# Sliding-window attention in float32: the value product written as three float32r passes over split operands, and a slope pass left out where its operand is zero

## What is computed

```python
def sliding_window_attention(q, k, v, sinks, slopes):
    # blocks of 128 tokens; kk and vv hold the previous block and this one
    logits = jnp.einsum('bnqkgd,bnskd->bnkgqs', qb, kk).astype(jnp.float32) * scale
    logits = logits - sl * dist.astype(jnp.float32)
    logits = jnp.where(valid[None, :, None, None], logits, -jnp.inf)
    p = jax.nn.softmax(jnp.concatenate([logits, sink], axis=-1), axis=-1)[..., :-1]
    out = jnp.einsum('bnkgqs,bnskd->bnqkgd', p.astype(v.dtype), vv)

def odd_layer(h, w_in, b_in, sinks, w_out):
    proj = h @ w_in + b_in
    q, k, v, g = jnp.split(proj, ODD_SPLITS, axis=-1)
    o = sliding_window_attention(q, k, v, sinks, alibi_slopes(SW_HEADS))
    return (o * jax.nn.silu(g)) @ w_out
```

## Time and profile before

| | us |
|---|---|
| median of 3 runs | 1840.45 (1839.17 to 1842.74) |
| the profiled execution, whole | 1845.26 |
| its span, first to last instruction | 1843.5 |
| PE busy | 1673.8 (91% of the span) |
| DVE busy | 1060.7 (58%) |
| ACT busy | 823.3 (45%) |
| the head loop: first scores to last value product | 1647 to 1768 |

### The profile page before, as it was taken

How to read it: one execution, slowest core, us unless ns; L and a number is a source line. 1 busy time by engine, 2 the same in 40 slices (tenths; PEclk the granted TensorE clock), 3 DMA queues, 4 the chain that set the end, 5 groups by cost and what they waited for, 6 DMA issues and landing times.

```text
span 1843.5 us, 24067 instructions
## 1 busy us (share of the span) xinstructions
PE 1673.8 (91%) x8860; PEld 1412.3 (77%) x8860; DVE 1060.7 (58%) x1760; ACT 823.3 (45%) x1544; POOL 93.4 (5%) x112
## 2 busy tenths in 40 slices
PE   7998999998999999989999998889987979979977
PEld 6886787886778888868798896668765758859965
DVE  5557877674545656552254438864465984446654
ACT  5545665663334455541132226652353542235641
POOL 2000400000000000000000001100000100000001
PEclk9998999999999999999999999988997989989988
DMA  6411122113431333322223320111320111320011
GB/s 184 125 50 30 46 63 64 46 52 110 141 120 47 101 104 91 91 92 67 99 74 99 108 81 25 35 46 41 102 84 21 47 46 47 99 69 24 28 42 46
DMA packets 147870, 132.95 MB, mean 72 GB/s; under 512 B 8560, under 2 KB 142448, under 8 KB 147776
## 3 DMA queue, kind: packets, MB, share of 16 engines
q1 hardware_dynamic: 143744, 119.58, 21.3%
q0 software_dynamic: 3136, 10.78, 1.6%
q10 hardware_dynamic: 896, 1.32, 0.3%
HBM read 124.33 MB, written 7.34 MB: 71 GB/s over the span
## 4 chain that ended last, share of the span: by engine, by line
PE 74%; DVE 15%; ACT 5%; issue 5%; DMA 1%; DVEq 0%; ACTq 0%; POOL 0%
PE bank L292 19%; PE bank L293 19%; PE bank L294 19%; DVE wlo L285 2%; PE bank L1206 2%; PE bank L1220 2%; ACT whi L278 1%; PE bank L1189 1%; PE bank L2911 1%; DVE ptl L1374 1%; DVE sz L2700 1%; PE bank L2870 1%; PE bank L1223 1%; PE bank L2278 1%; PE bank L2883 1%
## 5 line engine op out<-in xcount | busy, mean ns | idle before, releaser
L292 PE MATMUL bank<-hh,whi 128*128 128x512 f32 (+3 forms) x1208 | 466.2, 386 | 16.0 <-DVE wlo L285 5.6
L293 PE MATMUL bank<-hl,whi 128*128 128x512 f32 (+3 forms) x1208 | 455.7, 377 | 0.0
L294 PE MATMUL bank<-hh,wlo 128*128 128x512 f32 (+3 forms) x1208 | 455.2, 377 | 0.0
L278 ACT ACTIVATE whi<-wraw 128x2048 fp32r<-128x2048 f32 x111 | 212.1, 1913 | 338.6 <-PE bank L294 338.5
L285 DVE TENSOR_TENSOR wlo<-wraw,whi 128x2048 fp32r<-128x2048 f32 x111 | 254.1, 2289 | 178.7 <-ACT whi L278 177.3
L292 PEld LDWEIGHTS bank<-hh,whi 128*128 128x128 f32 (+2 forms) x1208 | 231.2, 191 | 60.9 <-issue 5.8
L294 PEld LDWEIGHTS bank<-hh,wlo 128*128 128x128 f32 (+2 forms) x1208 | 230.5, 191 | 43.3
L293 PEld LDWEIGHTS bank<-hl,whi 128*128 128x128 f32 (+2 forms) x1208 | 231.2, 191 | 39.1 <-issue 0.7
L1374 DVE TENSOR_TENSOR ptl<-bank,pth 128x128 fp32r<-128x128 f32 (+3 forms) x128 | 56.8, 485 | 64.4 <-ACT pth L1282 63.0
L292 PE MATMUL bank<-ah,whi 128*128 128x512 f32 (+1 forms) x224 | 83.8, 374 | 10.6 <-DVE al L3046 8.3
L292 PE MATMUL bank<-yh,whi 128*128 128x512 f32 (+1 forms) x220 | 79.3, 360 | 6.7 <-DVE yl L1740 6.7
(11 more groups left out here) (393 smaller groups left out, 3212.2 us busy)
## 6 DMA issues: line engine op xcount, KB each, us to landing
wraw<-in_w_in_a_dram SPq DMA_DIRECT2D x52, 512.0 KB, 4.5
wraw<-in_w_up_dram SPq DMA_DIRECT2D x42, 512.0 KB, 4.9
wraw<-in_w_in_dram SPq DMA_DIRECT2D x34, 512.0 KB, 4.8
wraw<-in_w_in_c_dram SPq DMA_DIRECT2D x18, 512.0 KB, 4.7
wraw<-in_w_down_dram SPq DMA_DIRECT2D x16, 512.0 KB, 4.0
wraw<-in_w_out_a_dram SPq DMA_DIRECT2D x16, 512.0 KB, 4.0
aside<-stage POOLq DMA_DIRECT2D x20, 256.0 KB, 2.3
wraw<-in_w_attn_br_dram SPq DMA_DIRECT2D x8, 512.0 KB, 4.0
```

The lines of the kernel that those rows point to most:

```text
L278: act.activation(whi[:, p], wraw[:, p], ACT.Copy).then_inc(w_hi_done, 1)
L292: pe.matmul(out, ws[0], hs[0], start=first, stop=False)
L293: pe.matmul(out, ws[0], hs[1], start=False, stop=False)
L294: return pe.matmul(out, ws[1], hs[0], start=False, stop=last)
```

## The change

Four edits:

1. The value product becomes three float32r passes. The values are written whole into `v3` by one DVE instruction; ACT copies them into `vph3` and DVE subtracts into `vpl3` (two instructions each); POOL zeroes only the columns between. The transposed probabilities are split as they leave PSUM: ACT copies bank 4 and then bank 5 into `pth3`, DVE subtracts each into `ptl3`. `values` waits for both subtractions and issues 12 matmuls in place of four.
2. `queries_low` moves on DVE ahead of the work on the transposed probabilities (`ptl3`), where it stood behind it (`pt3`).
3. The second slope pass and its diagonal are left out for the heads whose slope equals its high part (`exact`): the eight odd ones.
4. Two relays are dropped (`dt_v`, `k3_done`): DVE waited for its own result and then raised a semaphore for another engine, which now waits for the result's own semaphore. PE waits for `v3_pad` and `v3_low` ahead of the head loop, where DVE waited for `v3_pad`.

```diff
-            act.wait_ge(dt_v, 1)
+            act.wait_ge(drained, m0 + 13)
...
-            dve.wait_ge(drained, m0 + 13)
-            dve.sem_inc(dt_v, 1)
...
-            pool.memset(vp3[:, :, :], 0.0).then_inc(v3_pad, 1)
+            pool.wait_ge(drained, m0)
+            for part in (vph3, vpl3):
+                for a in range(0, 5 * HD, 2 * HD):
+                    ins = pool.memset(part[:, :, a:a + HD].bitcast(F32), 0.0)
+            ins.then_inc(v3_pad, 1)
...
-            pe.wait_ge(k3_done, 1)
+            pe.wait_ge(drained, m0 + 1)
...
             act.activation(dist3[:, :], dist3f[:, :], ACT.Copy).then_inc(c4_ready, 1)
+            act.wait_ge(drained, m0 + 2)
+            for g in range(2):
+                act.activation(vph3[:, :, HD + P * g:P + P * g], v3[:, :, HD * g:HD * g + HD], ACT.Copy) \
+                    .then_inc(v3_high, 1)
...
-            dve.wait_ge(drained, m0 + 1)
-            dve.sem_inc(k3_done, 1)
             split_lo(dve, n0 + 2)
             dve.wait_ge(tiles, 2 * n0 + 2)
-            dve.wait_ge(v3_pad, 1)
             dve.wait_ge(got_con, CON4)
-            for tt in range(TT):
-                dst = vp3[:, tt, HD:HD + 256].rearrange("p (g e) -> p g e", g=2)[:, :, 0:HD]
-                ins = dve.tensor_tensor(dst, bank[1][:, P * tt:P * tt + P].rearrange("p (g d) -> p g d", g=2),
-                                        bv3[:, :].rearrange("p (g d) -> p g d", g=2), ALU.add)
-            ins.then_inc(drained, 1)
+            dve.tensor_tensor(v3[:, :, :], bank[1][:, :].rearrange("p (t d) -> p t d", t=TT),
+                              bv3[:, :].unsqueeze(1).to_broadcast([P, TT, P]), ALU.add).then_inc(drained, 1)
+            for g in range(2):
+                cols = slice(HD + P * g, P + P * g)
+                dve.wait_ge(v3_high, g + 1)
+                dve.tensor_tensor(vpl3[:, :, cols], v3[:, :, HD * g:HD * g + HD], vph3[:, :, cols].bitcast(F32),
+                                  ALU.subtract).then_inc(v3_low, 1)
             dve.tensor_scalar(nsink[:, :], pcol("sinks", n=NH), -1.0, None, ALU.mult).then_inc(ns_done, 1)
             for g in range(2):
                 dve.wait_ge(kd3_done, g + 1)
@@ -2844,6 +2853,11 @@
         gated[0] += 1
         QB = NH // 2 + DA_H
...
+        TURNED = ((0, 0, 3 * P), (1, 3 * P, 4 * P))
+
+        def exact(h):
+            return high_part(sl[h]) == sl[h]
...
+            pe.wait_ge(v3_pad, 1)
+            pe.wait_ge(v3_low, 2)
...
-                    pe.matmul(out, dg3[:, h % 2, 0, :], dist3[:, lo:2 * P], start=False, stop=False)
-                    pe.matmul(out, dg3[:, h % 2, 1, :], dist3[:, lo:2 * P], start=False, stop=True).then_inc(s_done, 1)
+                    mm = pe.matmul(out, dg3[:, h % 2, 0, :], dist3[:, lo:2 * P], start=False, stop=exact(h))
+                    if not exact(h):
+                        mm = pe.matmul(out, dg3[:, h % 2, 1, :], dist3[:, lo:2 * P], start=False, stop=True)
+                    mm.then_inc(s_done, 1)
...
                     if i % 2 == 0 and h:
-                        pe.wait_ge(t3_dve if i else t3_act, h)
+                        pe.wait_ge(t3_dve, 2 * h if i else 2 * h - 1)
...
-                pe.wait_ge(t3_act, h + 1)
-                pe.wait_ge(t3_dve, h + 1)
+                pe.wait_ge(t3_dve, 2 * h + 2)
...
-                    mm = pe.matmul(bank[6][:, P * j:P * j + n], vp3[:, j, c0:c0 + P],
-                                   pt3[:, h % 2, 2 * P * j:2 * P * j + n], start=(e == 0 and j == 0),
-                                   stop=(e == 1 and j == TT - 1), skip_group_check=True)
+                    for v, p in ((vph3, pth3), (vpl3, pth3), (vph3, ptl3)):
+                        mm = pe.matmul(bank[6][:, P * j:P * j + n], v[:, j, c0:c0 + P],
+                                       p[:, h % 2, 2 * P * j:2 * P * j + n],
+                                       start=(e == 0 and j == 0 and v is vph3 and p is pth3),
+                                       stop=(e == 1 and j == TT - 1 and p is ptl3), skip_group_check=True)
                 mm.then_inc(pv_done, 1)
...
-                act.activation(dg3[:, h % 2, 0, :], ident[:, :], ACT.Copy, scale=hi_)
-                act.activation(dg3[:, h % 2, 1, :], ident[:, :], ACT.Copy, scale=sl[h] - hi_).then_inc(dg3_done, 1)
+                ins = act.activation(dg3[:, h % 2, 0, :], ident[:, :], ACT.Copy, scale=hi_)
+                if not exact(h):
+                    ins = act.activation(dg3[:, h % 2, 1, :], ident[:, :], ACT.Copy, scale=sl[h] - hi_)
+                ins.then_inc(dg3_done, 1)
...
                 if 1 <= h <= NH:
                     v = h - 1
-                    act.wait_ge(t_done, T3 + 2 * v + 1)
                     if v >= 2:
                         act.wait_ge(pv_done, V3 + v - 1)
-                    act.activation(pt3[:, v % 2, 0:3 * P], bank[4][:, 0:3 * P], ACT.Copy).then_inc(t3_act, 1)
+                    for b, c0, n in TURNED:
+                        act.wait_ge(t_done, T3 + 2 * v + b + 1)
+                        act.activation(pth3[:, v % 2, c0:c0 + n], bank[4 + b][:, 0:n], ACT.Copy).then_inc(t3_act, 1)
                 if h % 2 and h >= 3:
                     out_pair(h // 2 - 1)
                 if h % 2 == 0 and h // 2 + 1 < NH // 2:
@@ -3015,12 +3037,15 @@
                     for i in range(TT):
                         part = pr3[:, v % 2, i, (P if i == 0 else 0):2 * P]
                         dve.tensor_scalar(part, part, rs3[:, v % 2, i:i + 1], None, ALU.mult).then_inc(p_scaled, 1)
...
-                    dve.wait_ge(t_done, T3 + 2 * v + 2)
+                if h % 2 == 0 and h // 2 + 1 < NH // 2:
+                    queries_low(h // 2 + 1)
+                if 1 <= h <= NH:
                     if v >= 2:
                         dve.wait_ge(pv_done, V3 + v - 1)
-                    dve.tensor_copy(pt3[:, v % 2, 3 * P:7 * P], bank[5][:, :]).then_inc(t3_dve, 1)
-                if h % 2 == 0 and h // 2 + 1 < NH // 2:
-                    queries_low(h // 2 + 1)
+                    for b, c0, n in TURNED:
+                        dve.wait_ge(t3_act, 2 * v + b + 1)
+                        dve.tensor_tensor(ptl3[:, v % 2, c0:c0 + n], bank[4 + b][:, 0:n],
+                                          pth3[:, v % 2, c0:c0 + n].bitcast(F32), ALU.subtract).then_inc(t3_dve, 1)
                 if h % 4 == 1 and h > 1:
                     split_lo(dve, n0 + h // 4 + 1)
```

More of the change, by code:

```diff
@@ L2348, in two_blocks @@
     b_id, b_conv, b_silu = sem("b_id"), sem("b_conv"), sem("b_silu")
-    dt_v, dt_a, cs_done, cs_t, cs_tok, cl_mm, cl_exp = (
-        sem("dt_v"), sem("dt_a"), sem("cs_done"), sem("cs_t"), sem("cs_tok"), sem("cl_mm"),
+    dt_a, cs_done, cs_t, cs_tok, cl_mm, cl_exp = (
+        sem("dt_a"), sem("cs_done"), sem("cs_t"), sem("cs_tok"), sem("cl_mm"),
         sem("cl_exp"))
@@ L2760, in two_blocks @@
     sg3 = at("sg3", Y, [KT, S])
-    vp3 = at("vp3", Y + 52 * K, [TT, 320])
-    pt3 = at("pt3", Y + 58 * K, [2, 7 * P])
+    vph3 = at("vph3", Y + 52 * K, [TT, 320], F32R)
+    vpl3 = at("vpl3", SC_AT + 12 * K, [TT, 320], F32R)
+    v3 = at("v3", Y + 28 * K, [TT, P])
+    pth3 = at("pth3", Y + 58 * K, [2, 7 * P], F32R)
+    ptl3 = at("ptl3", SC_AT, [2, 7 * P], F32R)
     bv3 = at("bv3", Y + 66 * K, [P])
@@ L2775, in two_blocks @@
     nsink = at("nsink", S4 + 128, [NH])
-    k3_done, kd3_mm, kd3_done, v3_pad, c4_ready, ns_done = (
-        sem(n_) for n_ in ("k3_done", "kd3_mm", "kd3_done", "v3_pad", "c4_ready", "ns_done"))
+    v3_high, v3_low = sem("v3_high"), sem("v3_low")
+    kd3_mm, kd3_done, v3_pad, c4_ready, ns_done = (
+        sem(n_) for n_ in ("kd3_mm", "kd3_done", "v3_pad", "c4_ready", "ns_done"))
     dg3_done, t3_act, t3_dve, o3_out = (sem(n_) for n_ in ("dg3_done", "t3_act", "t3_dve", "o3_out"))
```

## The result

The changed kernel takes 1853.03 us (median of 10 runs, 1846.51 to 1855.78) against 1842.34 for the kernel before on the same chip (10 runs, 1839.17 to 1846.72). The medians lie 10.7 us apart. The ratio is 1.005, with a 95% interval of 1.0033 to 1.0066: slower by 0.5%, or 9.2 us (6.1 to 12.2). The profiled execution took 1853.29 us whole, 1851.5 from first to last instruction, 8.0 more than before.

The account below looks back on a forecast made before the run. PE was taken to bound the head loop at 6.905 us a head, and after the change a ring through PE, ACT and DVE; terms summed to +8.8 us, added to the median 1840.45: 1849.2 us, range 1841 to 1856.

Parts of the forecast that it names:

- the ring holds: Favoured case, 75%: a chain of waits through PE, ACT and DVE sets even iterations; own range 1846 to 1853 us.
- The ring: Even iterations, transposes through ACT's copies and high queries, DVE's low queries, subtractions, maxima and scaling: 8.13 us against 6.905.
- Where PE waits: Even iterations of the head loop: PE waits 0.4 us at the values, 1.4 us more at the next transposes.
- Iterations 6 and 10: Even iterations following a weight split on DVE: ACT is late, high queries start 0.40 us later; 8.53 us, 1.625 more than before.
- 5, 9 and 13: Odd iterations whose weight split follows the subtractions on DVE: split 0.65 us later, transposes at 7.34, +0.435 each.
- 3, 7 and 11: Odd iterations without queries: subtractions end before the new scores, so PE is bound; -0.09 us each.
- The value product: Twelve float32r matmuls per head on PE: 1.43 us, 0.09 less than the float32 product's 1.52.
- The slope pass: Leaving it out of an odd head saves PE 0.49 us, but inside PE's wait in even iterations gives nothing back.
- The end: Last values of the loop: ACT's copy comes first, then a subtraction as long as the old copy; +0.65 us.
- Outside the loop: Values' bias as one DVE instruction, -0.2 us; the two dropped relays, -0.1 us.
- The margin: Before the change, DVE's scaling ended only 0.27 us ahead of PE's next transposes, a thin reserve.
- The clock: Rival, 6%: PE's idling lowers its clock, +13 us in half the heads, 1862 us.

Follow-up runs that it names:

- the run with all slope passes: Changed kernel with the second slope pass issued for all heads again; ratio 1.006 (1.004 to 1.008) to the kernel before.
- the run with edit 3 alone: Kernel before with only the second slope pass and its diagonal left out for the eight odd heads; ratio 0.999 (0.998 to 1.0).
- order alone: Kernel before with only the low queries moved ahead of the copy of bank 5 on DVE; ratio 1.0007 (0.9994 to 1.002).
- three passes alone: Kernel before with the three-pass value product and dropped relays, low queries behind the subtractions, all slope passes kept; ratio 1.0011 (1.0 to 1.0022).

## Why the prediction was right

The forecast was +8.8 us, 1849.2, within 1841 to 1856; the runs give +9.2 by the ratio (1853.03 as a median). Of the 3.8 us between 1849.2 and the median, 1.9 are the kernel before, whose median of 10 runs is 1842.34 and not the 1840.45 of the three that I had; 0.4 are the change, and the rest is that the medians differ by 10.7 and the ratio says 9.2. The case that the ring holds came in. That the ratio and the loop both say 9.2 is partly luck, since the ratio's interval is 6 us wide; the mechanism rests on the stages in the traces.

- **The ring.** Forecast 8.13 us from transposes to transposes, measured 8.18. Link by link, forecast and measured after the opening: high queries 1.45 and 1.48, low queries 2.74 and 2.77, subtractions 4.05 and 4.19, maxima 5.21 and 5.26, next transposes 8.13 and 8.18. The largest miss is 0.14: DVE took the first subtraction only after the last low query had ended, where I had taken its start from a row that overlaps. The next maxima did start 0.09 before the subtractions ended (1687.02 + 1.16 against 1688.09), as the sum had it.
- **Where PE waits.** Forecast 0.4 us ahead of the values and 1.4 us ahead of the transposes. In iteration 4 the last gate matmul started at 1687.54, the first value matmul at 1688.23, 0.46 later than the 0.23 steps of such matmuls would have it:

```profile
1687.54 0.39 PE L294 MATMUL bank<-hh,wlo 128*128 128x512 f32 x1
1688.23 0.39 PE L2929 MATMUL bank<-pth,vph 128*128 128x256 f32 x1 [0.30 <-DVE ptl L3047]
```

The other wait is 1.17 by its bracket, with modelled ends, and 8.18 - 6.31 - 0.46 = 1.4 by the starts.
- **Iterations 6 and 10**, forecast 8.53: 8.53. In iteration 6 high queries started at 1.81 (forecast 1.85), low ones at 3.12, subtractions at 4.54. **5, 9 and 13**, forecast 7.34: 7.42; in iteration 5 the weight split started at 2.30, forecast 2.22, and 0.05 of the 0.08 us are the transposes, which again take longer right behind the scaling. **3, 7 and 11**, forecast 6.82: 6.78. **14**, forecast 6.34: 6.31. Over the 14 iterations the forecast was 8.53 us more (the sum's terms without iteration 1, the end and the parts outside the loop), the trace has 103.58 - 94.83 = 8.75.
- **The value product** was mis-sized: 1.43 forecast, 1.34 measured, in these rows of iteration 3 (the first and the last three of the twelve, and the transposes behind):

```profile
1681.49 0.28 PE L2929 MATMUL bank<-pth,vph 128*128 128x256 f32 x1
...
1682.54 0.22 PE L2929 MATMUL bank<-pth,vph 128*128 128x128 f32 x1
1682.60 0.27 PE L2929 MATMUL bank<-pth,vpl 128*128 128x128 f32 x1
1682.71 0.27 PE L2929 MATMUL bank<-ptl,vph 128*128 128x128 f32 x1
1682.83 0.95 PE L2901 MATMUL bank<-ident,pr 128*128 128x128 f32 x7
```

Nine wide ones took 1.05 us (0.117 each) and the three narrow ones 0.29. The 1.14 us that three quarters of the float32 product would be was not reached even here. The steps suggest why (no run isolates it): 0.11 between narrow matmuls and 0.12 between wide ones, so the product pays for each matmul rather than for its columns. The Trainium skill, page "TensorE: Matmul & The Clock Gate", section "LDWEIGHTS (loading the stationary operand)", puts a weight load at the number of its columns divided by 1.2 GHz, 107 ns for 128; the 0.11 us steps agree with that. They do so at a granted clock of 1.00 only: in the run with all slope passes the clock was 0.50 from 1655.2 to 1660.2 us, and the scores started 0.21 us apart at 128 columns (1657.06 to 1657.27) as at 256 (1658.23 to 1658.44).
- **The slope pass** gives back nothing inside the wait: shown by the run with all passes (0.49 us, all of it in iteration 14) and, from the other side, by the run with edit 3 alone (0.47 for an even iteration).
- **The end**, forecast +0.65 for the wait of the last values. They started 1773.87 - 1771.45 = 2.42 us after the last transposes, against 1765.94 - 1764.14 = 1.80 before: +0.62. Their product is shorter, so the end is only 0.46 us longer (4.67 or 4.68 against 4.21) in all six kernels with three passes. The forecast put 0.65 in full on the path and left the shorter product out.
- **Outside the loop**, forecast -0.3: the next matmul of PE started 0.74 us after DVE began on the values' bias (1615.69 to 1616.43), 0.93 before: -0.19 of the forecast -0.2. This is one trace of each kernel. The two relays can't be told from the scatter ahead of the loop; no run isolates them.
- **The margin** of 0.27 us was no reading of a plain iteration: it is that of iteration 5, and iteration 4 has 0.54 (see the slope pass left out alone). No term of the sum for iterations 2, 4, 8 and 12 uses it.
- **The clock** stayed at 1.00 from 1680 to 1760 us in spite of PE's waits, as in rows 11, so that rival is out.

Not seen in the prediction: how far the loss was from necessary. I took the ring as the price of the change, while moving one half of the queries' split to the other iteration turns +9.2 into -3.0.

## What to carry to other kernels

When two engines split an operand between them, write the order of both lists side by side: an instruction that waits for something late in the other's list holds up everything behind it, and the price is that of the whole loop through both lists, not of the instruction (here 7.1 us for the place of two kinds of instructions on DVE). Look for such a ring before counting busy time, and cut it by issuing the early link an iteration ahead, while the other engine would be idle. What is saved on an engine that waits within the same iteration is worth nothing until the wait has gone; so price edits together, and check an edit's worth again once the bound has moved.

## What the runs showed of the hardware

- Three float32r matmuls in place of one in float32 are worth 0.16 us of 1.5 for a product of 896 columns in blocks of 256 and 128, since the float32r ones start 0.11 to 0.12 us apart at both widths. Behind the first narrow one the next starts after 0.06 us (one product's rows).
- The start of the head loop has two forms in the traces of these kernels. Where the first seven transposes took 1.75 or 1.76 us (six kernels and the one before), iteration 1 took 9.6 to 9.8 us; where they took 1.15 to 1.19 (slope pass alone, order alone, three passes alone), 8.4 to 8.5. In the changed kernel the granted clock of 1658 to 1668 us was 0.68, so the transposes and scores behind PE's first wait ran at the lower level. In the 5 us from the first transposes on, the clock was 0.50 in the first form and 0.66 in the second, and PE had been idle for 3.30 to 3.87 us ahead of them in the first and 2.73 to 3.20 in the second. The 1.2 us between the forms are part of the scatter of whole times.
